# Mixture-of-experts stage: experts ranked by rows on chip, three of them in two products per weight tile, and a seventh of the weight splits on GpSimd

## The chip, the cores and the metric
One core of a Trainium2 chip (trn2). The time is the device time of one execution in microseconds; the kernel before has a median of 1638.44 us over three runs.

## What is computed
The kernel runs a trunk of two layers over 256 rows of 1024 numbers, all in float32. Each layer has an attention, a cross-attention to 256 memory rows and a feed-forward part, each followed by a layer norm of `ALPHA * x + sublayer(x)`. The change lies in the last feed-forward part, the experts of layer 1:

```python
def swiglu(x, w_gate, w_up, w_down):
    return (jax.nn.silu(x @ w_gate) * (x @ w_up)) @ w_down

def moe_swiglu(x, router, w_gate, w_up, w_down):
    logits = (x @ router).astype(jnp.float32)
    top_vals, top_idx = lax.top_k(logits, TOP_K)
    gates = jax.nn.softmax(top_vals, axis=-1)
    combine = jnp.sum(jax.nn.one_hot(top_idx, N_EXPERTS, dtype=jnp.float32) * gates[..., None], axis=-2)
    y = jnp.zeros_like(x)
    for e in range(N_EXPERTS):
        y = y + combine[..., e:e + 1].astype(x.dtype) * swiglu(x, w_gate[e], w_up[e], w_down[e])
    return y
```

There are 8 experts, each row takes the best 2 of them, and an expert has three matrices of 1024 x 3584 (the last one transposed): 44.04 MB in float32.

## The kernel before, in words
**Products in two halves.** A float32 matrix is split into a high half (`hi`, rounded to float32r) and a low half (`lo` = value - `hi`). A product is the sum of three matmuls: x_hi with w_hi, x_hi with w_lo, x_lo with w_hi (L397 to L399).

**Chunks.** Weights come in chunks of 1 MB: 128 partitions x 4 tiles of 512 columns. An expert has EC = 42 chunks: 28 for gate and up (EJ = 7 column blocks, two chunks of gate and two of up each), then 14 for down (7 for each half of y's 1024 columns). For each chunk SP issues the DMA into one of seven `raw` buffers (NEXP = 7; L921, once the low half of the chunk seven earlier is made), ACT makes `w_hi` by a copy (L1116), DVE makes `w_lo` by a subtraction (L1964, `w_split` in DVE's `expert`), and PE runs 12 matmuls of 128x512.

**Slots.** The halves lie in four slots (`E_SLOT`), except for the chunks 20 to 25, which go round in three. `E_SPLIT[c]` lists the chunks whose halves may be made once PE has used chunk c: c + 4, or 3 later near there. ACT waits for `chunk_used`, DVE for `hi_made`, PE for `lo_made`; every engine goes through its own instructions in order.

**Jobs.** One job is one expert; `expert(job, z)` is written once for each engine as the body of a loop and once more, with z = "z", for the last job. A job takes up to 128 rows of its expert; where one expert has more, a second round of 8 jobs follows (`rounds`). The rows are placed by prefix sums (`place`), and a one-hot matrix `pick` (L1855) selects them. At chunk 4 (`C_INDEX`) PE forms the row numbers of the next job, DVE copies them (`got_i`, L1467), POOL gathers the rows (`get_x`, L1077), and at chunk 32 (`C_TURN`) PE turns them and ACT and DVE split them into `xe_hi` and `xe_lo` (L1869). For each column block j ACT computes silu of gate (`e_g`, L1420), DVE multiplies by up (`e_h`, L1957), PE transposes (L864), and ACT and DVE split the result into `eT_hi` and `eT_lo` (L1973). y is copied by ACT and stored by a DMA into `y_rows` (L1432).

**Last job.** DVE works out the row numbers of all rows' two results (`row_numbers`, L1890 to L1907), POOL gathers them from `y_rows` in four pairs (`get_y`, L1086, each pair after DVE has added the one before), and DVE adds them to x (`add_got`, L1932) at the chunks 12, 16, 20 and 24. The last job's own y is combined by PE (L819) and added by DVE (`add_last`, L1941). The final layer norm and the store of the output follow. Its parameters `gb` are loaded by POOL's `ln_params(5)` before the experts.

**GpSimd (POOL).** Ahead of the experts it makes five `w_lo` by the same subtraction (`split`, L1010), masks for the attention (L945) and, in layer 0, fills a part of `y_rows` with x by 10 DMAs of 512 KB so that unused rows hold numbers (L1027).

Of the kernel before, what the change touches and what calls it, by code (L numbers as in the profile page):

```python
# [26 lines left out]
P = 128  # L27
# [4 lines left out]
def trunk(nc, x, mem, ln_g, ln_b, mem_wq, mem_wkv, mem_wo, ab_w_in, ab_sinks, ab_w_out,  # L32
# [77 lines left out]

    with ExitStack() as ctx:
# [88 lines left out]
        eT_lo = at("eT_lo", [P, EK, P], F32R, o_region + 4 * EK * P)  # L200
        o = o_region + 8 * EK * P
# [10 lines left out]
        xe_lo = at("xe_lo", [P, KT, P], F32R, o_xt + 4 * KT * P)  # L212
        e_h = [at(f"e_h{i}", [P, W], F32, o_scr + 4 * W * i) for i in range(2)]
# [9 lines left out]
        for name, shape, dt in (  # L223
# [17 lines left out]
        taken, place, most, rounds = (small[n] for n in ("taken", "place", "most", "rounds"))  # L241
        token_no, got_i, mine, nth, late = (
            small[n] for n in ("token_no", "got_i", "mine", "nth", "late"))
        fin, is_fin, w_fin, last_job = (small[n] for n in ("fin", "is_fin", "w_fin", "last"))
# [39 lines left out]
        for n in range(NSPL + 1, EC + NSPL + 1):  # L284
            at_step = max(at_step, max(m for m in range(-EC, n) if E_SLOT[m % EC] == E_SLOT[n % EC]))
            E_SPLIT[at_step].append(n)
        C_GOT = {12 + 4 * n: (n // TB, n % TB) for n in range(2 * TB)}
        C_INDEX, C_TURN, C_COMBINE = 4, 4 * EJ + 4, 4 * EJ + EK // CK + 2
# [76 lines left out]
        def _(pe):  # L365
            pair = [0]

            def chunk_product(c, outs, lhs_hi, lhs_lo, k0, first, last, cols, idx=None, slot=None,
                              rows=None, done=None, ready=None, turned=False):
# [3 lines left out]
                pe.wait_ge(lo_made, c + 1 if idx is None else idx + 1)  # L373
# [435 lines left out]
            pe.wait_ge(sem("rounds_made"), 2)  # L809
            last = pe.value_load(last_job[0:1, 0:1], min_val=NE - 1, max_val=2 * NE - 1)  # L810
# [12 lines left out]
            def expert(job, z):  # L823
                start = list(claims)
                for c in range(EC):
# [4 lines left out]
                    if c == C_INDEX:  # L830
                        pe.wait_ge(sem("picked"), job + 2)
                        if z:

                            d = claim(pe, "pT", 5, job)
# [3 lines left out]
                        else:  # L838
                            index("iB", job)
                    if c < 4 * EJ:  # L840
                        j, q = c // 4, c % 4
                        key, b = (f"{z}eg{j}", j % 2) if q < 2 else (f"{z}eu{j}", 2 + j % 2)
                        if q % 2 == 0:
                            claim(pe, key, b, job, signal=False)
                        chunk_product(c, [(0, bank[b])], xe_hi, xe_lo, 4 * (q % 2), q % 2 == 0,
                                      q % 2 == 1, W, idx=idx, slot=E_SLOT[c], done=chunk_used)
                    else:
# [3 lines left out]
                        if i == 0:  # L851
# [3 lines left out]
                                      q == EK // CK - 1, W, idx=idx, slot=E_SLOT[c],  # L855
                                      done=chunk_used)
                    if c % 4 == 1 and 1 <= c // 4 <= EJ:
# [5 lines left out]
                        for q in range(4):  # L863
                            m = nc.tensor.transpose(d[:, q * P:(q + 1) * P],  # L864
                                                    e_h[j % 2][:, q * P:(q + 1) * P], ident[:, :])
                        m.then_inc(filled[b], 1)
                    if c == C_TURN and not z:

                        pe.wait_ge(sem("x_got"), 16 * job + 16)
                        turn("xB", job)  # L870
                    if z and c in (C_COMBINE, EC - 1):
# [7 lines left out]
            assert [a - b for a, b in zip(claims, before[0])] == JOB_CLAIMS  # L879
# [6 lines left out]
        def _(sp):  # L886
# [45 lines left out]
            with sp.Else():  # L932
                sp.nop()
# [1121 lines left out]
```

## Time and profile before

| | |
|---|---|
| three runs | 1637.53, 1638.44, 1640.66 us; median 1638.44 |
| profiled execution: span from first to last instruction | 1639.8 us |
| its own time | not listed beside the span; the span stands for it |
| first expert chunk on PE | about 666 us |
| last matmul of the last expert chunk | about 1625 us |
| busy: PE / DVE / ACT / POOL | 1599.7 / 1259.6 / 1029.8 / 121.1 us |
| moved by DMA | 481.24 MB, mean 293 GB/s |

Busy times are sums over the span, and matmuls overlap, so a busy PE only says that it never ran dry. The granted clock of PE is given as a share of full speed: 1.00 is 2.4 GHz, 0.50 is 1.2 GHz. A span of 2.29 us of one DVE instruction contains a start-up that the next one overlaps.

### The profile page before, as it was taken

The numbers are of one execution on the slowest core, as the hardware profiler recorded it, in microseconds if no ns is written. First come the engines' busy times: TensorE is split into PE (matmuls) and PEld (weight loads), VectorE is DVE, ScalarE is ACT, GpSimd is POOL, SyncE is SP. The second block draws the span as 40 slices with busy tenths as digits, with TensorE's granted clock in tenths as the row PEclk, the third lists the DMA queues.
The fourth block names the chain that finished last, engine by engine and source line by source line (L and its number), as shares of the span: only waits on it lengthen the run. The fifth ranks groups of instructions, "written<-read, shape, count | busy, mean of one in ns | idle before, by whom it ended". The sixth has DMA issues, their size and how long they took to land.

```text
span 1639.8 us, 22497 instructions
## 1 busy us (share of the span) xinstructions
PE 1599.7 (98%) x8202; PEld 1347.1 (82%) x8202; DVE 1259.6 (77%) x1173; ACT 1029.8 (63%) x920; POOL 121.1 (7%) x131
## 2 busy tenths in 40 slices
PE   9999999999999998999999999999999999999996
PEld 8888988888896796888888888888888888888775
DVE  4687475554647656889889889888988988988996
ACT  4564444343437454677777777777777777777673
POOL 2103010000104101000000000000000000000120
PEclk9999999999999999999999999999999999999999
DMA  9437656466455363899999999999999999999992
GB/s 351 164 127 252 213 182 216 128 219 200 161 193 185 135 206 105 318 364 377 389 363 385 389 364 375 389 371 384 388 368 387 388 358 386 388 362 389 359 369 94
DMA packets 238397, 481.24 MB, mean 293 GB/s; under 512 B 8256, under 2 KB 11360, under 8 KB 238336
## 3 DMA queue, kind: packets, MB, share of 16 engines
q1 hardware_dynamic: 229744, 454.06, 77.3%
q0 software_dynamic: 6576, 22.68, 4.1%
q10 hardware_dynamic: 2016, 3.67, 0.6%
q8 instruction: 40, 0.66, 0.2%
q14 instruction: 21, 0.17, 0.0%
HBM read 474.07 MB, written 11.56 MB: 296 GB/s over the span
## 4 chain that ended last, share of the span: by engine, by line
PE 84%; DVE 9%; issue 2%; DMA 2%; ACT 2%; POOL 1%; POOLq 0%; DVEq 0%; SPq 0%; ACTq 0%
PE bank L397 23%; PE bank L399 23%; PE bank L398 23%; PE bank L387 3%; PE bank L390 3%; PE bank L389 3%; DVE w_lo L1483 2%; PE bank L864 1%; DVE w_lo L1964 1%; DMA y_got<-y_rows,row_i 1%; PE bank L684 1%; PE bank L660 1%; DVE X L1520 1%; ACT w_hi L1116 1%; DVE X L1529 1%
## 5 line engine op out<-in xcount | busy, mean ns | idle before, releaser
L1116 ACT ACTIVATE w_hi<-raw 128x2048 fp32r<-128x2048 f32 (+1 forms) x322 | 608.8, 1895 | 258.7 <-PE bank L399 220.3
L1964 DVE TENSOR_TENSOR w_lo<-raw,w_hi 128x2048 fp32r<-128x2048 f32 x221 | 503.1, 2290 | 81.8 <-ACT w_hi L1116 78.5
L1483 DVE TENSOR_TENSOR w_lo<-raw,w_hi 128x2048 fp32r<-128x2048 f32 (+1 forms) x96 | 211.2, 2204 | 145.5 <-ACT w_hi L1116 145.2
L397 PE MATMUL bank<-w_hi,xe_hi 128*128 128x512 f32 x736 | 292.9, 398 | 1.2 <-DVE w_lo L1964 1.2
L399 PE MATMUL bank<-w_hi,xe_lo 128*128 128x512 f32 x736 | 287.9, 391 | 0.0
L398 PE MATMUL bank<-w_lo,xe_hi 128*128 128x512 f32 x736 | 287.4, 390 | 0.0
L399 PEld LDWEIGHTS bank<-w_hi,xe_lo 128*128 128x128 f32 x736 | 138.5, 188 | 29.9
L397 PEld LDWEIGHTS bank<-w_hi,xe_hi 128*128 128x128 f32 x736 | 138.6, 188 | 28.8 <-DVE w_lo L1964 1.6
L398 PEld LDWEIGHTS bank<-w_lo,xe_hi 128*128 128x128 f32 x736 | 138.8, 189 | 27.4
L1964 DVE TENSOR_TENSOR w_lo_more<-raw,w_hi_more 128x2048 fp32r<-128x2048 f32 x63 | 144.2, 2290 | 18.5 <-ACT w_hi_more L1116 11.4
L397 PE MATMUL bank<-w_hi,xT_hi 128*128 128x512 f32 (+1 forms) x384 | 147.0, 383 | 0.1
L399 PE MATMUL bank<-w_hi,xT_lo 128*128 128x512 f32 (+1 forms) x384 | 144.5, 376 | 0.0
L398 PE MATMUL bank<-w_lo,xT_hi 128*128 128x512 f32 (+1 forms) x384 | 144.5, 376 | 0.0
L1116 ACT ACTIVATE w_hi_more<-raw 128x2048 fp32r<-128x2048 f32 x64 | 122.9, 1920 | 28.0 <-PE bank L399 23.8
L397 PE MATMUL bank<-w_hi,eT_hi 128*128 128x512 f32 x320 | 125.8, 393 | 0.5 <-DVE w_lo L1964 0.5
L399 PE MATMUL bank<-w_hi,eT_lo 128*128 128x512 f32 x320 | 124.6, 390 | 0.0
L398 PE MATMUL bank<-w_lo,eT_hi 128*128 128x512 f32 x320 | 124.6, 389 | 0.0
L387 PE MATMUL bank<-xT_hi,w_hi 128*128 128x256 f32 x352 | 101.1, 287 | 2.1 <-DVE w_lo L1483 2.1
L389 PE MATMUL bank<-xT_lo,w_hi 128*128 128x256 f32 x352 | 100.3, 285 | 0.0
L390 PE MATMUL bank<-xT_hi,w_lo 128*128 128x256 f32 x352 | 100.3, 285 | 0.0
L1964 DVE TENSOR_TENSOR w_lo<-raw_more,w_hi 128x2048 fp32r<-128x2048 f32 x40 | 91.4, 2286 | 3.7 <-ACT w_hi L1116 3.7
L1116 ACT ACTIVATE w_hi<-raw_more 128x2048 fp32r<-128x2048 f32 x40 | 76.7, 1916 | 25.0 <-PE bank L399 25.0
(291 smaller groups left out, 2598.4 us busy)
## 6 DMA issues: line engine op xcount, KB each, us to landing
raw<-in_moe_w_gate_dram SPq DMA_DIRECT2D x96, 1024.0 KB, 9.2
raw<-in_moe_w_up_dram SPq DMA_DIRECT2D x96, 1024.0 KB, 8.4
raw<-in_moe_w_down_dram SPq DMA_DIRECT2D x96, 1024.0 KB, 7.2
raw<-in_mem_wkv_dram SPq DMA_DIRECT2D x16, 1024.0 KB, 5.1
raw_more<-in_moe_w_up_dram SPq DMA_DIRECT2D x16, 1024.0 KB, 8.7
raw_more<-in_moe_w_gate_dram SPq DMA_DIRECT2D x16, 1024.0 KB, 8.7
raw_more<-in_moe_w_down_dram SPq DMA_DIRECT2D x16, 1024.0 KB, 7.8
raw<-in_c_w_in_dram SPq DMA_DIRECT2D x12, 1024.0 KB, 5.2
```

The lines of the kernel that those rows point to most:

```text
L387: nc.tensor.matmul(d, wh, xh, start=(first and k == 0 and q % 2 == 0), stop=False, skip_group_check=True)
L389: nc.tensor.matmul(d, wh, xl, start=False, stop=False, skip_group_check=True)
L390: m = nc.tensor.matmul(d, wl, xh, start=False, stop=(last and k == n - 1), skip_group_check=True)
L397: nc.tensor.matmul(d, xh, hi[:, k, :], start=(first and k == 0), stop=False)
L398: nc.tensor.matmul(d, xh, lo[:, k, :], start=False, stop=False)
L399: m = nc.tensor.matmul(d, xl, hi[:, k, :], start=False, stop=(last and k == n - 1))
L660: m = nc.tensor.matmul(d[:, t * SEQ:(t + 1) * SEQ], QK[:, 2 * h + k, t * P:(t + 1) * P], MK[:, 2 * h + k, :], start=(k == 0), stop=(k == 1))
L684: m = nc.tensor.matmul(d[:, k * SEQ:(k + 1) * SEQ], MV[:, mb, c:c + P], PT_t[i % 2][:, mb * SEQ:(mb + 1) * SEQ], start=(mb == 0), stop=(mb ...
L864: m = nc.tensor.transpose(d[:, q * P:(q + 1) * P], e_h[j % 2][:, q * P:(q + 1) * P], ident[:, :])
L1116: return nc.scalar.activation(dst, src, ACT.Copy)
L1483: tt(w_lo[s][:, 0:n], raw[c % NRAW][:, 0:n], w_hi[s][:, 0:n].bitcast(F32), ALU.subtract).then_inc(lo_made, 1)
L1964: tt(w_lo[s][:, :], raw_exp[r][:, :], w_hi[s][:, :].bitcast(F32), ALU.subtract).then_inc(lo_made, 1)
```

## The change
Four things change; the arithmetic stays within the same scheme.

1. **Ranking.** The number of rows of each of the experts 1 to 7 is counted and ranked on DVE (`count`, `sort_key`, `above`, `rank`, `ranked`); `room` is 64 rows for the three with fewest and 128 otherwise. If all fit (`most` = 0) there are 8 jobs: expert 0 and two wide ones in a loop (WIDE = 3), then twice a pair of a narrow and a wide job (PAIRS = 2), then the last job, narrow. If one doesn't fit, 8 more wide jobs go ahead. SP reads the experts' numbers from `sorted_e`.
2. **Narrow jobs.** The 64 rows' high and low halves stand side by side in the 128 columns of one stationary tile (`xe_two`, `eT_two`), and a weight tile takes two matmuls, with w_hi and with w_lo. The halves of the result are added afterwards: for gate and up by a product with a folding matrix (`fold`), for y by DVE.
3. **GpSimd** makes `w_lo` of the chunks 5, 12, 19, 26, 33 and 40 of each job (`POOL_SPLITS`), from two tiles in SBUF, with a semaphore of its own.
4. **Around it.** `ln_params(5)` moves behind POOL's last split, `y_rows` is filled whole (16 DMAs of 512 KB, not 10), a narrow y is stored with 64 rows and later, and DVE's `row_numbers` grows.

```diff
+    HP = P // 2
+    NARROW, PAIRS = 3, 2
+    WIDE = NE - NARROW - PAIRS
+    ORDER = [0, 1, 4, 2, 5, 3, 6]
+        POOL_SPLITS = [n for n in range(NSPL + 1, EC) if n % NEXP == NEXP - 2]
@@ PE, chunk_product
-                pe.wait_ge(lo_made, c + 1 if idx is None else idx + 1)
+                pe.wait_ge(*((lo_made, c + 1) if idx is None else split_done(c, job)))
+                    if packed is not None:
+                        d, two = outs[0][1][:, 0:cols], packed(k0 + k)
+                        nc.tensor.matmul(d, two, hi[:, k, :], start=(first and k == 0), stop=False)
+                        m = nc.tensor.matmul(d, two, lo[:, k, :], start=False, stop=(last and k == n - 1))
+                        continue
@@ PE, expert
+                            if narrow:
+                                for src, col in ((e_g[j % 2], q * HP), (e_h[j % 2], W // 2 + q * HP)):
+                                    m = nc.tensor.matmul(d[:, col:col + HP], src[:, q * P:(q + 1) * P],
+                                                         fold[:, :], start=True, stop=True,
+                                                         skip_group_check=True)
-            with pe.Fori(0, last) as job:
-                expert(job, "")
-            expert(last, "z")
+            with pe.Fori(0, wide) as job:
+                expert(job, "", False)
+            with pe.Fori(0, PAIRS) as i:
+                job = pe.snap(wide + 2 * i)
+                expert(job, "n", True)
+                expert(job + 1, "w", False)
+            expert(wide + 2 * PAIRS, "z", True)
@@ SP
-                        sp.wait_ge(lo_made, N0 + c - NEXP + 1 + EC * job)
+                        sp.wait_ge(*split_done(c - NEXP, job))
+            for r in range(NR):
+                e = sp.value_load(sorted_e[0:1, r:r + 1], min_val=0, max_val=NE - 1)
+                expert_chunks(e, more + (r + 1))
@@ POOL
-                        for r in range((NE - 2) * P, 2 * NE * P, SEQ):
+                        for r in range(0, 2 * NE * P, SEQ):
-            ln_params(5)
+            def w_split(n, job):
+                r, s = n % NEXP, E_SLOT[n % EC]
+                pool.wait_ge(hi_made, N0 + n + 1 + EC * job)
+                nc.gpsimd.tensor_tensor(w_lo[s][:, :], raw_exp[r][:, :], w_hi[s][:, :].bitcast(F32),
+                                        ALU.subtract).then_inc(sem("lo_by_pool"), 1)
+            def next_x(job):
+                w_split(POOL_SPLITS[0], job)
                 pool.wait_ge(sem("index_made"), job + 1)
                 pool.sem_inc(sem("x_asked"), 1)
                 get_x()
+                for n in POOL_SPLITS[1:]:
+                    w_split(n, job)
+            late_splits = {0: POOL_SPLITS[1:2], 1: POOL_SPLITS[2:3], 2 * TB - 1: POOL_SPLITS[3:]}
             for g in range(2 * TB):
                 get_y(g)
+                for n in late_splits.get(g, ()):
+                    w_split(n, last)
+            pool.wait_ge(chunk_used, EC * wide + (N0 + 4 * EJ + EC * 2 * PAIRS))
+            pool.dma_start(gb[:, 0, :], ln_g[LNS[5]].partition_broadcast(P)).then_inc(sem("ln_in"), 16)
@@ ACT, expert, narrow
+                            copy(e_g[j % 2][:, :], bank_of(f"{z}eg{j}")[:, :])
+                        copy(e_h[j % 2][:, :], bank_of(f"{z}eu{j}")[:, :]).then_inc(sem("e_hidden"), 1)
+                            nc.scalar.activation(e_act[j % 2][:, :], b[:, 0:W // 2], ACT.Silu)\
+                        act.wait_ge(sem("e_mult"), EJ * n_narrow + j + 1)
+                        copy(eT_two[:, 4 * j:4 * j + 4, 0:HP],
+                             e_mul[j % 2][:, :].rearrange("p (k s) -> p k s", k=4))\
@@ DVE, expert
+                        if n in POOL_SPLITS:
+                            return
+                        copy(y[0:HP, col], b[HP:P, :]).then_inc(sem(f"y_low{i}"), 1)
+                        tt(y[0:HP, col], b[0:HP, :], y[0:HP, col], ALU.add).then_inc(sem(f"y_made{i}"), 1)
+                        tt(e_mul[j % 2][:, :], bank_of(f"{z}et{j}")[:, W // 2:W], e_act[j % 2][:, :], ALU.mult)\
+                        empties(tt(eT_two[:, 4 * j:4 * j + 4, HP:P],
+                                   e_mul[j % 2][:, :].rearrange("p (k s) -> p k s", k=4),
+                                   eT_two[:, 4 * j:4 * j + 4, 0:HP].bitcast(F32), ALU.subtract), f"{z}et{j}")
@@ DVE, turned
+                        tt(xe_two[:, 4 * half:4 * half + 4, HP:P],
```

## Rows read from the trace of the kernel before
**Rows 1.** The page's busy shares, and its chain that ended last, by engine.
```profile
PE 1599.7 (98%) x8202; PEld 1347.1 (82%) x8202; DVE 1259.6 (77%) x1173; ACT 1029.8 (63%) x920; POOL 121.1 (7%) x131
...
PE 84%; DVE 9%; issue 2%; DMA 2%; ACT 2%; POOL 1%; POOLq 0%; DVEq 0%; SPq 0%; ACTq 0%
```

**Rows 2.** Windows: us; PE, PEld, DVE, ACT, POOL busy us (x); PEclk; DMA share; GB/s.
```profile
907.08:1026.09 119.01, 119.01 (x545) 98.62 (x545) 104.79 (x61) 90.19 (x61) 2.67 (x1) 1.00 1.03 376
1499.00:1625.50 126.50, 122.40 (x539) 98.69 (x537) 111.13 (x96) 83.52 (x57) 18.09 (x8) 0.99 0.85 313
```

**Rows 3.** Timeline of PE (start us, us, instruction): every third matmul, first and last.
```profile
938.54 0.39 PE L397 MATMUL bank<-w_hi,xe_hi 128*128 128x512 f32 x1
...
942.62 0.39 PE L397 MATMUL bank<-w_hi,xe_hi 128*128 128x512 f32 x1
```

**Rows 4.** Windows with DMA's share and GB/s, experts first, then the fills of layer 0.
```profile
690.00:720.00 30.00, 30.00 (x139) 24.81 (x138) 27.09 (x18) 22.19 (x16) 1.08 (x1) 1.00 1.05 387
892.00:960.00 68.00, 68.00 (x311) 56.31 (x310) 59.75 (x35) 51.90 (x36) 2.67 (x1) 1.00 1.05 388
...
165.00:180.00 15.00, 15.00 (x122) 14.87 (x122) 7.22 (x4) 7.58 (x6) 0.00 (x0) 1.00 1.03 365
180.00:200.00 20.00, 19.70 (x110) 17.29 (x109) 11.10 (x25) 9.85 (x24) 0.00 (x0) 1.00 0.25 91
```

**Rows 5.** Timeline of DVE in one job.
```profile
974.18 0.68 DVE L1957 TENSOR_TENSOR e_h<-bank,e_g 128x512 f32<-128x512 f32 x1
975.09 2.29 DVE L1964 TENSOR_TENSOR w_lo<-raw,w_hi 128x2048 fp32r<-128x2048 f32 x1 [0.22 <-DVE e_h L1957]
...
997.04 0.69 DVE L1973 TENSOR_TENSOR eT_lo<-bank,eT_hi 128x512 fp32r<-128x512 f32 x1
997.64 4.49 DVE L1964 TENSOR_TENSOR w_lo<-raw,w_hi 128x2048 fp32r<-128x2048 f32 x2
```

**Rows 6.** POOL's splits and DVE's L1520: ns min/median/max by line; timeline of 412 to 418.
```profile
L1010 POOL TENSOR_TENSOR w_lo<-raw,w_hi x5: 4607/4612/4617, 136.6 to 634.3; 128x2048 fp32r<-128x2048 f32 x5
...
L1520 DVE SCALAR_TENSOR_TENSOR X<-X,mean_var,gb x10: 1265/1266/1801, 142.0 to 644.7; 128x1024 f32<-128x1024 f32 x10
...
412.40 4.61 POOL L1010 TENSOR_TENSOR w_lo<-raw,w_hi 128x2048 fp32r<-128x2048 f32 x1 [174.61 <-ACT w_hi L1116]
...
414.33 0.69 DVE L1505 SCALAR_TENSOR_TENSOR X<-X,bank 128x512 f32<-128x512 f32 x1 [7.14 <-PE bank L399]
415.05 0.69 DVE L1509 BATCH_NORM_STATS2 stats<-X 128x6 f32<-128x512 f32 x1
...
416.29 1.80 DVE L1520 SCALAR_TENSOR_TENSOR X<-X,mean_var,gb 128x1024 f32<-128x1024 f32 x1
```

**Rows 7.** POOL's selects by line; timeline of POOL, then DVE, 501 to 505.
```profile
L945 POOL TENSOR_SCALAR_AFFINE_SELECT c_add<-c_add x32: 283/295/2332, 461.9 to 538.8; 128x128 f32<-128x128 f32 x32
...
502.36 2.28 POOL L945 TENSOR_SCALAR_AFFINE_SELECT c_add<-c_add 128x128 f32<-128x128 f32 x2 [1.83 <-DMA c_add<-gate_rows]
...
501.95 2.29 DVE L1483 TENSOR_TENSOR w_lo<-raw,w_hi 128x2048 fp32r<-128x2048 f32 x1 [1.06 <-ACT w_hi L1116]
```

**Rows 8.** Timeline of POOL, then DVE, in the last job: gathers of y.
```profile
1546.43 3.01 POOL L1086 DMA_INDIRECT y_got<-y_rows,row_i  x1 [27.38 <-DVEq L1935]
...
1558.59 3.01 POOL L1086 DMA_INDIRECT y_got<-y_rows,row_i  x1 [6.95 <-DVEq L1935]
...
1569.14 0.75 DVE L1932 SCALAR_TENSOR_TENSOR X<-y_got,g,X 128x512 f32<-128x512 f32 x1 [1.36 <-DMA y_got<-y_rows,row_i]
```

**Rows 9.** Windows of the end, and the chain in order of time from the last matmul.
```profile
1605.00:1610.00 5.00, 5.00 (x24) 4.14 (x23) 4.05 (x3) 4.15 (x3) 0.00 (x0) 1.00 0.21 77
...
1625.22 0.24 PE bank L399
```

**Rows 10.** Windows around the router's stage.
```profile
643.50:647.40 3.90, 0.05 (x1) 0.00 (x0) 3.66 (x10) 0.20 (x1) 0.11 (x1) 0.90 0.34 137
647.40:653.30 5.90, 5.61 (x26) 3.84 (x27) 3.16 (x6) 5.11 (x6) 1.58 (x3) 0.50 0.51 160
```

More of the change, by code:

```diff
@@ L200, in trunk @@
         eT_lo = at("eT_lo", [P, EK, P], F32R, o_region + 4 * EK * P)
+        eT_two = at("eT_two", [P, EK, P], F32R, o_region)
+        e_act = [at(f"e_act{i}", [P, W // 2], F32, o_region + 4 * EK * P + 2 * W * i) for i in range(2)]
+        e_mul = [at(f"e_mul{i}", [P, W // 2], F32, o_region + 4 * EK * P + 4 * W + 2 * W * i) for i in range(2)]
         o = o_region + 8 * EK * P
@@ L821, in combine, with expert @@
                         .then_inc(filled[2 * half + t], 1)
-            def expert(job, z):
+            def expert(job, z, narrow):
+                claims[:], signals[:] = before[0], before[1]
                 start = list(claims)
+                last = z == "z"
                 for c in range(EC):
@@ L845, in expert @@
                         chunk_product(c, [(0, bank[b])], xe_hi, xe_lo, 4 * (q % 2), q % 2 == 0,
-                                      q % 2 == 1, W, idx=idx, slot=E_SLOT[c], done=chunk_used)
+                                      q % 2 == 1, W, idx=idx, slot=E_SLOT[c], done=chunk_used, job=job,
+                                      packed=(lambda k: xe_two[:, k, :]) if narrow else None)
                     else:
@@ L1391, in turned @@
                     b = wait_filled(act, f"{tag}{half}", job)
+                    if job is not None:
+                        copy(xe_two[:, 4 * half:4 * half + 4, 0:HP],
+                             b[:, :].rearrange("p (k s) -> p k s", k=4)[:, :, 0:HP])
                     copy(xe_hi[:, 4 * half:4 * half + 4, :].rearrange("p k s -> p (k s)"), b[:, :])\
@@ L1396, in _, with expert @@
             split(N0 + NSPL)
-            act.wait_ge(sem("rounds_made"), 2)
-            last = act.value_load(last_job[0:1, 0:1], min_val=NE - 1, max_val=2 * NE - 1)
+            act.wait_ge(sem("jobs_made"), 2)
+            wide = act.value_load(n_wide[0:1, 0:1], min_val=WIDE, max_val=WIDE + NE)
             assert cursor[0] == N0 + NSPL + 1
-            def expert(job, z):
+            def expert(job, z, narrow, n_narrow=None):
+                last = z == "z"
                 nc.scalar.preload_act_table_set("silu_and_others")
@@ L1945, in add_last, with last_picks, expert @@
                 link(ins)
-            def expert(job, z):
+            def last_picks():
+                for t in range(TB):
+                    for a in (0, HP):
+                        ins = nc.vector.tensor_scalar(pick[:, t, a:a + HP], slot_no[:, 0:HP],
+                                                      place[:, t, 3 * NE - 1:3 * NE], None, ALU.is_equal)
+                ins.then_inc(sem("picked"), 1)
+            def expert(job, z, narrow, n_narrow=None):
+                last = z == "z"
                 for c in range(EC):
                     idx = N0 + c + EC * job
-                    if c < 4 * EJ and c % 4 == 3:
+                    if not narrow and c < 4 * EJ and c % 4 == 3:
                         j = c // 4
@@ L1977, in expert @@
                     if c == 0:
[L1979 to L1980 removed]
+                        if last:
+                            last_picks()
+                        else:
+                            picks(bass.ds(job + (NE + 1), 1))
+                    if c == C_INDEX + 1 and last:
                         b = wait_filled(dve, "pT", job)
```

302 lines of the change are left out of this document (216 added, 86 removed).

## Prediction
> **What bounds the kernel now.** I read the page's shares first: PE is busy for 98% of the span, DVE for 77% [rows 1], and PE has 84% of the chain that ended last [rows 1]. Stages differ, so next the windows: from 668 us on the experts run, one job (one expert) like the other, 119.01 us each. In one such job PE has no idle time, DVE is busy 104.79 us, ACT 90.19, POOL 2.67, and DMA moves 376 GB/s at a share of 1.03 [rows 2]. So PE sets the pace, but DVE has only 14 us to spare. The matmul rows give PE's price: 18 of them in 4.08 us, 0.227 each [rows 3]; 12 a chunk and 42 chunks are 114.4 us, the rest of the 119 are transposes. The third limit is DMA. Over long stretches in which every buffer is asked for as soon as it is free, it moves 387 to 388 GB/s at a share of 1.05, and no longer stretch shows more [rows 4]. A job needs 44.0 MB of weights, 0.5 MB of gathered x and 0.5 MB of stored y: 45.1 MB / 388 GB/s = 116.2 us. DMA is thus 3 us a job behind PE. Three limits lie at 119, 116 and 105 us; the change lowers the first by far and moves the last.
>
> **Does it do what it says?** Worked through the reference with its inputs, the experts get 67, 65, 53, 55, 61, 62, 80, 69 rows. The three smallest of experts 1 to 7 (53, 55, 61) fit into 64 rows and the rest into 128, so there are again 8 jobs, in the order wide, wide, wide, narrow, wide, narrow, wide, narrow. A count too large would add 8 jobs; it isn't so here.
>
> **PE, narrow jobs.** 8 matmuls in place of 12 a chunk: 42 x 8 x 0.227 = 76 us, and with 56 products by fold and the turn about 84, against 119. From PE alone three such jobs would give back 105 us. None of it counts below the next limit: 44.8 MB (half a y) / 388 = 115.5 us by DMA.
>
> **DVE and POOL.** Every job gives 6 of its 42 w_lo splits to POOL. On DVE one costs 2.20 us back to back (two in 4.49, one in 2.29) [rows 5]; on POOL 4.61 us, five of five [rows 6]. As work beside DVE this would take 6 x 2.20 = 13 us from DVE. But the rows speak against "beside". While POOL's split ran from 412.40 to 417.01, a DVE operation with two SBUF inputs (L1520) that began at 416.29 took 1.80 us, where the other nine took 1.27: it ended 1.08 us after POOL did. The two just before it, with an input from a bank or with one input, kept their 0.69 [rows 6]. The other way round, POOL's selects of c_add have a median of 0.295 us but up to 2.33, and a pair took 2.28 us while a w_lo of DVE ran from 501.95 to 504.24, the first of them waiting until that was over [rows 7]. So an operation that reads two SBUF tiles and one of POOL that reads SBUF exclude each other for their whole length; w_lo reads raw and w_hi, both in SBUF. This is how the Trainium skill has it (SBUF — State Buffer, "Who interferes with whom"): VectorE's second input comes through the interface that GpSimd uses, and whoever starts second is blocked until the first is done; these rows agree. By that rule the sum is the one below; without it, it is rival A's.
>
> The price in DVE's stream: from the end of one w_lo POOL needs 4.61 less the 0.19 that a blocked operation has already behind it (1.27 - 1.08), 4.42, and the next w_lo ends 2.10 later; that is 6.52 for what took 4.40, +2.12 us a split, +12.7 a job. The offload costs DVE's stream time instead of giving it any. Wide job: 104.8 + 12.7 + 0.7 (two xe_two parts) = 118.2 us against PE's 119.0. Narrow: 36 x 2.20 + 6 x 4.33 = 105.2; e_mul and eT_two, 128x256 each, in place of e_h and eT_lo of 128x512, which hold the stream for 0.91 and 0.60 [rows 5]: half the columns, some 0.34 each, 14 of them 4.8; turn 1.9; y's low half by copy and add 3.2; picks and index 0.6: 115.7, with a few tenths of waiting 117, beside DMA's 115.5. ACT, with the same 42 splits and some halves more, stays near 95.
>
> **Where waits appear.** A split starts when PE has used the chunk 4 earlier (3 earlier for chunks 23 to 28). Wide, 4 slots: 1.9 (ACT) + 4.6 + 0.2 = 6.7 us within 3 x 2.72 = 8.2, mostly covered, with DVE's lag behind it down to some tenths. Wide, 3 slots (chunk 26, POOL's): 6.8 within 2 x 2.72 + 0.5 (transposes) = 5.9: PE waits 0.9 us a job, where DVE's split fits (4.4). Queued behind DVE's blocked w_lo are e_h and eT_lo, which PE's transposes wait for.
>
> **The sum against the span.** (a) Router: DVE has 6 more small linked operations at 0.2 us before its next split and 9 after the first ones, the latter under PE's first chunks: +0.5; bounds 0 and +3. (b) Jobs 0 to 2, wide: 120.0 each, +3; bounds 0 (all covered) and +12 (DVE's lag reaches PE in each cycle of seven). (c) First narrow: 117, and PE, which ends a wide job 3.8 us behind its last w_lo, ends this one 2 behind: 115.2, -3.8; twice, -7.6; bounds -18 (more of POOL's time under DVE's bank operations, DMA's 115.5 the limit, the full lead given back) and +2. (d) The two wide jobs between start without lead: 119.0 + 0.9 + some 1.6 until the lead is there, +2.5 each, +5; bounds 0 and +8. (e) Last job, narrow: before, 126.5 us, DVE busy 111.1 of them [rows 2] and, in its own order, occupied from the first split to the last. To its stream of 116.4 come 12.7 for POOL, some 13 row-number operations (+2.8), from it go 5.6 (e_h, eT_lo): 126.3. POOL is also asked for y_got here; between two gathers now stands a split. The gathers already follow each other at 12 us, and DVE once waited 1.36 for one [rows 8]; adding 4.6 to that chain costs 2 to 5 us. 131, +4.5; bounds -2 and +10. (f) From the last matmul to the end: 14.3 us [rows 9], unchanged; the layer norm's gb is now fetched behind POOL's last split, 9 us ahead of its use; bounds 0 and +2. (g) Six more y_rows fills early (10 of 512 KB before): DMA is full there until 180 us and then falls to a share of 0.25 [rows 4], and the weights run six buffers ahead: 0; bounds 0 and +3. POOL issues them in 3.4 us, and its next work waited 4.2.
> Sum: 0.5 + 3 - 7.6 + 5 + 4.5 = +5.4. The span of 1639.8 gives 1645.2; the three runs' median of 1638.4 lies 1.4 below that span, so 1643.8, rounded to 1644.
>
> **Rivals.** A, POOL works beside DVE (its w_lo doesn't hold back DVE's): then DVE has 92 us a job, the narrow ones run at DMA's pace and PE's lead over the landing data (DMA falls silent near 1606, PE works to 1625 [rows 9]), 19 us down to 7, is given back once: first narrow -15.5, second -6.3, last -7.7, wide ones +5, router +0.5: -24, 1614. For it: only one pair with POOL's split overlaps in this trace; against it: that pair, and the selects that waited [rows 7]. B, exclusion holds but is absorbed, since 118.2 is still under 119.0 and 115.7 under it too: wide 0, narrow -9.2 and -4, wide between +0.9 each, last +0.5: -11, 1627. It decides if PE's idle time in the wide jobs stays under 0.3 us. C, heavier: every POOL split holds up PE by 0.5 us in wide jobs (5 x 3), narrow jobs gain nothing, last +10: +25 and more, 1664. To it belongs the clock: after 3.9 us without matmuls PE ran at a granted 0.50, that is 1.2 of 2.4 GHz, for 6 us [rows 10]; in narrow jobs PE pauses some 2.5 us at each POOL split, and at that level a chunk needs 3.6 us instead of 1.8. The sign between my case and B hangs on two or three us of stalls, so neither is remote.
>
> **Numbers.** My case 0.46, B 0.22, A 0.15, C 0.12, the small rest between A and B. The range reaches from just under A to the lower part of C: 1613 to 1657; my case alone is 1639 to 1651. A measurement of this kernel can tell 0.2% (3.3 us) from no change: faster (under 1635.2) 0.36, from A, B and the rest; same 0.20, from the edges of my case and B; slower 0.44.
>
> **What would show it.** Right: DVE rows of w_lo with up to 6.7 us beside POOL's 4.6, POOL rows above 4.61 where a w_lo ran, narrow jobs of about 117 us with PE's matmuls near 70% of them, wide jobs of 120, PE waiting for POOL's w_lo. Wrong: w_lo staying at 2.29 us during POOL's splits (A); narrow jobs clearly under 114 us, which would say that DMA can move over 388 GB/s; wide jobs of 123 or PEclk falling in the narrow ones (C).

## The result, and the profile after

Median of four runs 1691.74 us (1690.04 to 1694.52) against 1637.99 (1636.16 to 1640.66) for the kernel before on the same chip: ratio 1.0329, interval 1.0311 to 1.0347. The change makes the kernel 3.3% slower. The profiled execution has a span of 1688.8 us. The forecast of 1644, its range up to 1657 and even rival C (1664) were all too low.

The page of after, shares and chain [rows 1]:

```profile
PE 1558.9 (92%) x7950; PEld 1298.1 (77%) x7950; DVE 1297.8 (77%) x1176; ACT 1040.5 (62%) x972; POOL 362.2 (21%) x196
...
PE 50%; issue 22%; DVE 15%; POOL 7%; ACT 4%; DMA 1%; ACTq 0%; DVEq 0%; POOLq 0%
```

PE has 252 matmul records fewer and yet fell from 98% to 92% of a longer span; its share of the last chain fell from 84% to 50%. DVE lost 48 of its w_lo operations to POOL and is busy 38 us *more* (1297.8 against 1259.6; the same kernel without POOL's splits, experiment 1, has 1261.4). The same in windows, one for each job (columns as in [rows 2]; the jobs are wide, wide, wide, narrow, wide, narrow, wide, narrow, as the prediction worked them out):

```profile
663.40:792.09 128.69, 123.50 (x549) 101.64 (x548) 108.49 (x67) 91.00 (x64) 32.91 (x7) 0.97 0.92 331
...
916.71:1041.31 124.60, 121.11 (x545) 99.71 (x545) 106.36 (x57) 90.88 (x63) 32.91 (x7) 0.99 1.00 362
1041.31:1165.74 124.43, 101.02 (x456) 78.84 (x456) 112.67 (x59) 92.05 (x76) 30.41 (x7) 0.93 0.99 359
1165.74:1295.42 129.68, 124.05 (x549) 101.22 (x547) 110.36 (x61) 91.15 (x64) 33.39 (x7) 0.97 1.01 362
```

A wide job that took 119.01 us now takes 124.6: PE is idle for 3.5 of it, and its 545 matmuls are busy for 121.1 where they were for 119.0, mostly by a slower clock, shown below; a narrow job, with a third fewer matmuls on its weights (456 of all kinds against 545), takes 124.4 and leaves PE idle for 23. Nothing is at its limit there: DMA moves 359 GB/s where it could move 387 [rows 4], DVE is busy 113 us of 124. It is waits. After's lines by source say how the operations changed (ns min/median/max):

```profile
L2179 DVE TENSOR_TENSOR w_lo<-raw,w_hi x189: 2274/2283/6662, 669.6 to 1663.5; 128x2048 fp32r<-128x2048 f32 x189
...
L2179 DVE TENSOR_TENSOR w_lo<-raw_more,w_hi x40: 2276/3919/5436, 676.0 to 1646.8; 128x2048 fp32r<-128x2048 f32 x40
...
L1169 POOL TENSOR_TENSOR w_lo<-raw,w_hi x32: 4516/4624/6124, 669.0 to 1664.9; 128x2048 fp32r<-128x2048 f32 x32
...
L1992 DVE TENSOR_SCALAR pick<-slot_no,place x16: 273/280/4600, 655.0 to 1429.8; 128x128 f32<-128x128 f32 x16
```

The first three are the exclusion as predicted: w_lo up to 6.66 us beside POOL, POOL up to 6.12 beside w_lo. The fourth was not predicted: a comparison of 128 columns that takes 0.28 us takes up to 4.60. Where it stands, in the timeline of a wide job:

```profile
922.17 4.79 DVE L1992 TENSOR_SCALAR pick<-slot_no,place 128x128 f32<-128x128 f32 x2
...
922.29 4.57 POOL L1169 TENSOR_TENSOR w_lo<-raw,w_hi 128x2048 fp32r<-128x2048 f32 x1 [14.76 <-ACT w_hi L1210]
...
926.88 2.28 DVE L2179 TENSOR_TENSOR w_lo<-raw_more,w_hi 128x2048 fp32r<-128x2048 f32 x1
...
927.09 0.60 PE L835 MATMUL bank<-token_no,pick 128*128 128x1 f32 x4 [2.68 <-DVE pick L1992]
```

The picks of chunk 0 (the next job's rows) are issued right behind the w_lo of chunk 4, and POOL's first split of a job, chunk 5, starts 0.12 us after them. The second pick waits until POOL is done, and in PE's queue the index product sits ahead of the experts' matmuls: PE waits 2.68 us. Two microseconds later the granted clock is at 0.50, which is where most of the 2.1 us of longer matmuls come from (with the picks moved, experiment 3, it is 119.5 at a clock of 1.00):

```profile
929.00:931.00 2.00, 2.00 (x6) 1.56 (x5) 1.77 (x3) 0.00 (x0) 0.00 (x0) 0.50 1.05 386
```

In a narrow job PE is further ahead:

```profile
1046.77 4.73 DVE L1992 TENSOR_SCALAR pick<-slot_no,place 128x128 f32<-128x128 f32 x2
...
1051.63 1.01 PE L835 MATMUL bank<-token_no,pick 128*128 128x1 f32 x4 [5.82 <-DVE pick L1992]
```

and the granted clock falls, windows of the same job:

```profile
1051.00:1056.00 5.00, 4.37 (x12) 3.67 (x13) 4.90 (x3) 0.17 (x1) 0.42 (x1) 0.50 1.05 388
1056.00:1061.00 5.00, 5.00 (x26) 4.26 (x25) 2.29 (x1) 3.60 (x3) 0.00 (x0) 0.74 1.05 387
```

After 5.8 us without a matmul of the experts PE runs at 0.50, that is 1.2 GHz, as after the 3.9 us of [rows 10], and does 12 matmuls in 5 us. PE's waits from 700 to 1670 us (us in total, times, longest):

```profile
PE bank L420 <- DVE w_lo L2179: 24.3, 18, 4.5
PE bank L835 <- DVE pick L1992: 21.5, 6, 5.8
PE bank L420 <- POOL w_lo_more L1169: 9.3, 6, 2.3
PE bank L420 <- DVE eT_two L2195: 9.0, 3, 3.0
PE bank L420 <- DVE w_lo_more L2179: 7.0, 2, 6.5
PE bank L881 <- DVE pick L2142: 6.1, 1, 6.1
...
PE bank L439 <- POOL w_lo L1169: 4.0, 5, 0.8
```

L420 is the narrow jobs' first product, L439 the wide ones'. In before the longest entry of this view is 2.3 us in all. The first entry, 24.3 us, is for the most part not the splits' doing: without them (no_pool) it is still 18.9 us in 18 waits. The pick's 21.5 us are 1.8 there.

### The profile page after: what moved, and what is told of

Read it like the earlier page. It is cut to its first block, busy times and chain, and to the rows that moved or that the text cites. A ratio compares the mean times of both kernels' runs of the same rounds, so it can differ in the third digit from the quotient of the medians.

```text
span 1688.8 us, 22163 instructions
## 1 busy us (share of the span) xinstructions
PE 1558.9 (92%) x7950; PEld 1298.1 (77%) x7950; DVE 1297.8 (77%) x1176; ACT 1040.5 (62%) x972; POOL 362.2 (21%) x196
## 4 chain that ended last, share of the span: by engine, by line
PE 50%; issue 22%; DVE 15%; POOL 7%; ACT 4%; DMA 1%; ACTq 0%; DVEq 0%; POOLq 0%
PE bank L439 11%; PE bank L441 11%; PE bank L440 11%; DVE w_lo L2179 4%; POOL w_lo L1169 3%; PE bank L429 3%; PE bank L432 3%; PE bank L431 3%; ACT w_hi L1210 2%; POOL w_lo_more L1169 2%; DVE w_lo L1620 2%; PE bank L420 1%; DVE w_lo_more L2179 1%; PE bank L421 1%; DVE pick L1992 1%
## 5 line engine op out<-in xcount | busy, mean ns | idle before, releaser
L2179 DVE TENSOR_TENSOR w_lo<-raw,w_hi 128x2048 fp32r<-128x2048 f32 x189 | 440.0, 2351 | 62.2 <-ACT w_hi L1210 59.8
L1169 POOL TENSOR_TENSOR w_lo<-raw,w_hi 128x2048 fp32r<-128x2048 f32 x32 | 157.3, 4916 | 404.2 <-ACT w_hi L1210 404.2
L439 PE MATMUL bank<-w_hi,xe_hi 128*128 128x512 f32 x460 | 186.6, 406 | 4.0 <-POOL w_lo L1169 4.0
L441 PE MATMUL bank<-w_hi,xe_lo 128*128 128x512 f32 x460 | 182.8, 397 | 0.0
L440 PE MATMUL bank<-w_lo,xe_hi 128*128 128x512 f32 x460 | 182.7, 397 | 0.0
L439 PE MATMUL bank<-w_hi,xT_hi 128*128 128x512 f32 (+1 forms) x384 | 147.0, 383 | 0.1
L420 PE MATMUL bank<-w_hi,xe_two 128*128 128x512 f32 x276 | 120.4, 436 | 18.1 <-DVE w_lo L2179 10.7
L1169 POOL TENSOR_TENSOR w_lo_more<-raw,w_hi_more 128x2048 fp32r<-128x2048 f32 x16 | 81.3, 5081 | 212.6 <-ACT w_hi_more L1210 212.6
L421 PE MATMUL bank<-w_lo,xe_two 128*128 128x512 f32 x276 | 115.3, 418 | 0.9 <-issue 0.9
L439 PEld LDWEIGHTS bank<-w_hi,xe_hi 128*128 128x128 f32 x460 | 88.7, 193 | 22.9 <-POOL w_lo L1169 5.2
L441 PEld LDWEIGHTS bank<-w_hi,xe_lo 128*128 128x128 f32 x460 | 88.5, 192 | 19.4
L440 PEld LDWEIGHTS bank<-w_lo,xe_hi 128*128 128x128 f32 x460 | 88.8, 193 | 17.8
```

The lines of the kernel that those rows point to most:

```text
L420: nc.tensor.matmul(d, two, hi[:, k, :], start=(first and k == 0), stop=False)
L421: m = nc.tensor.matmul(d, two, lo[:, k, :], start=False, stop=(last and k == n - 1))
L439: nc.tensor.matmul(d, xh, hi[:, k, :], start=(first and k == 0), stop=False)
L440: nc.tensor.matmul(d, xh, lo[:, k, :], start=False, stop=False)
L441: m = nc.tensor.matmul(d, xl, hi[:, k, :], start=False, stop=(last and k == n - 1))
L1169: nc.gpsimd.tensor_tensor(w_lo[s][:, :], raw_exp[r][:, :], w_hi[s][:, :].bitcast(F32), ALU.subtract).then_inc(sem("lo_by_pool"), 1)
```

## Experiments

Two theories. **Theory 1**: POOL's splits cost the time, because POOL and DVE keep each other out of SBUF; the narrow products alone are a gain. **Theory 2**: the rest of the change (ranking, narrow jobs, their order on DVE) costs it. Ratios are to the kernel before on the same chip.

**1. no_pool**: after, with no split on POOL.

```
-POOL_SPLITS = [n for n in range(NSPL + 1, EC) if n % NEXP == NEXP - 2]
+POOL_SPLITS = []
```

> The changed kernel with all low halves of the experts on DVE again; ranking and narrow jobs stay. Theory 1 (POOL's splits and DVE's two-input operations exclude each other, and that is what the change costs): DVE's w_lo rows are all 2.29 us, the first narrow job takes about 116 us by DMA less some lead, the wide ones 119, and the time falls from 1691.7 to about 1614 us, under the kernel before. Theory 2 (the narrow form costs: its longer chain ACT-DVE-PE, pauses and PE's clock): narrow jobs stay at 123 us or more and the time stays over 1660.

Measured: 1616.97 us (1614.99 to 1619.18), ratio 0.9857, interval 0.9839 to 0.9874. Two of its jobs, wide and narrow, in windows:

```profile
904.32:1023.38 119.06, 119.06 (x546) 98.63 (x545) 105.45 (x63) 90.73 (x63) 2.68 (x1) 1.00 1.03 376
1023.38:1133.88 110.50, 100.57 (x472) 78.82 (x471) 103.51 (x67) 93.12 (x75) 2.54 (x1) 0.97 1.05 388
```

Wide jobs are back at 119.06, PE without a gap; the narrow one ends at DMA's 388 GB/s. Six splits more on DVE, and DVE is busy 9 us *less* in the narrow job than in after. The change without POOL's splits is worth 1.4%; the splits cost 4.8% beside it (1.0329 / 0.9857).

**2. before_pool**: the kernel before, plus POOL's six splits of a job and nothing else of the change. The first stands ahead of the gather of x and the rest behind it, DVE passes these chunks over, and PE and SP wait for whoever makes a chunk.

```
+                w_split(POOL_SPLITS[0], job)
...
+                for n in POOL_SPLITS[1:]:
+                    w_split(n, job)
...
+                        if n in POOL_SPLITS:
+                            return
```

> The kernel before with nothing but POOL's six splits a job. Theory 1: each wide job costs what it costs in the changed kernel, 124.6 us in place of 119.0, eight jobs give +45 and with the gathers of the last one some +50: about 1685 us. Theory 2: within 5 us of the kernel before, 1638.

Measured: 1687.09 us (1680.33 to 1697.63), ratio 1.0302, interval 1.0253 to 1.0351. The splits cost the old kernel 3.0%. Its jobs 1 to 4 take 123.0 us instead of 119.0, jobs 5 and 6 124.6, the last 138.4 instead of 123.3. Two of these jobs in windows:

```profile
911.08:1034.07 122.99, 119.50 (x546) 98.58 (x545) 105.09 (x55) 90.36 (x61) 32.30 (x7) 1.00 1.01 367
1280.01:1404.60 124.59, 121.12 (x545) 99.74 (x545) 105.05 (x55) 90.37 (x62) 32.26 (x7) 0.99 1.00 362
```

PE waits 16.0 us in six for the picks, 2.7 each. After the same 2.7 us the granted clock stayed at 1.00 in the first of the two and fell to 0.50 in the second, which makes it 1.6 us longer; why it fell in one and not in the other no run shows. The time met the expected 1685, but not by its sum: the expectation had 124.6 for every wide job, five of seven had 123.0, and the last job lost 15.1 us, more than was put down for it. Theory 2 falls, as it does by experiment 1. Alone the splits cost 3.0%, beside the narrow jobs 4.8%.

**3. picks_first**: after, with the picks of chunk 0 ahead of the w_lo of chunk 4 on DVE, to keep them away from POOL's split. Is the pick a tenth of the loss or most of it?

```
+                    if c == 0:
+                        if last:
+                            last_picks()
+                        else:
+                            picks(bass.ds(job + (NE + 1), 1))
                     if not narrow and c < 4 * EJ and c % 4 == 3:
...
-                    if c == 0:
-                        if last:
...
```

> The changed kernel with DVE's picks of chunk 0 ahead of w_lo of chunk 4 in place of behind it, so that they are not queued beside POOL's split of chunk 5. In the profile of the changed kernel the picks take 4.8 us in place of 0.48 and PE waits 2.7 (wide) to 5.8 us (narrow) for them. Theory 1a (the picks are the main place of the cost): PE's waits at the index are gone, with the slow clock behind them, 5 x 3 + 3 x 8 us: about 1655 us. Theory 1b (DVE's stream is full, so the stall only moves to the next operation behind the split): at most 10 us faster, 1682 or more.

Measured: 1662.73 us (1660.98 to 1666.32), ratio 1.0135, interval 1.0119 to 1.0152. The placement of two operations of 0.28 us a job is worth some 30 of the 75 us between after and no_pool (the ratios give 1.9%). A wide and a narrow job:

```profile
912.66:1032.93 120.27, 119.46 (x545) 98.49 (x545) 106.76 (x57) 90.90 (x63) 34.92 (x7) 1.00 1.02 375
1032.93:1149.17 116.24, 99.69 (x454) 77.33 (x454) 108.66 (x58) 92.14 (x75) 32.34 (x7) 0.96 1.04 380
```

120.27 and 116.24, where the prediction had 120.0 and 115.2. The time still lies 8 us over 1a's value. One reason is that the move does not clear the picks everywhere: in jobs 0 and 4 the first pick meets POOL's split all the same and takes 4.18 and 4.69 us, and PE waits 2.1 and 1.9. What else is left stands in the table below.

**4. before_pool_picks**: the same move in the version of experiment 2, where nothing of the narrow jobs disturbs the reading.

> The kernel before with GpSimd's six splits (1687) and VectorE's picks of chunk 0 issued ahead of its low half of chunk 4. Theory 1a (the picks, held for GpSimd's split of chunk 5, keep TensorE 2.7 to 3 us a job, and that is most of what a split costs a wide job): jobs of 120.0 in place of 123.0, over eight jobs about 24 less, 1658 to 1668. Theory 1b (the low halves that are late cost the time, whoever is blocked first): over 1678.

Measured: 1657.09 us (1655.45 to 1662.59), ratio 1.0121, interval 1.0097 to 1.0145: 1a, a touch under its band. Here no pick takes over 0.29 us. Jobs 1 to 6 take 120.2 or 120.3 us each:

```profile
905.56:1025.82 120.26, 119.45 (x546) 98.50 (x545) 105.46 (x55) 90.37 (x62) 34.28 (x7) 1.00 1.03 374
```

So a wide job's 4.0 us were 2.8 for the picks and 1.2 for all six splits together; the last job, 132.5 us instead of 123.3, still pays 9.2. Over the run the 48 splits cost 18 us here (1657.1 against 1639.1), 0.4 each.

**5. half**: after, with three splits a job on POOL (chunks 12, 26, 40), none near the picks.

```
+POOL_SPLITS = [12, 26, 40]
...
                 get_x()
-                for n in POOL_SPLITS[1:]:
+                for n in POOL_SPLITS:
```

> The kernel after, but GpSimd makes the low halves of chunks 12, 26 and 40 alone (three a job in place of six, none of them near the picks of chunk 0, and each behind the gather of x). Theory 1c: each split of GpSimd costs the same wherever it stands, because for its 4.6 us it and VectorE's low halves keep each other out; between the version without them (1617) and the one with six and the picks moved ahead (1663) three lie in the middle: about 1640 (1633 to 1648), VectorE's low halves beside them about 6.7 us, and no pick over 0.6 us. Theory 2c: it is the split of chunk 5, close behind the start of the job, that does the harm, and VectorE has slack for the others: 1617 to 1627.

Measured: 1637.97 us (1633.8 to 1641.74), ratio 0.9989, interval 0.9976 to 1.0002. With 0, 24 and 48 splits (the last with the picks moved) the medians are 1617.0, 1638.0 and 1662.7: 0.88 and 1.03 us a split. Theory 1c's time came, and of the numbers tried none is free: with three a job all that the narrow jobs bring is spent. Its reason, the same cost wherever a split stands, did not: against no_pool the three splits cost a wide job 1.0 us, the first narrow job 2.5 and the last job 7.3 (table below), and in the kernel without narrow jobs a split cost 0.4 (experiment 4).

**6. pool_writes and pool_copy**: what in POOL's operation keeps DVE out? In the first POOL fills its six w_lo with zeros (it writes and reads nothing); in the second it copies raw to w_lo (one input). Both leave the subtraction out for six chunks of 42.

```
-nc.gpsimd.tensor_tensor(w_lo[s][:, :], raw_exp[r][:, :], w_hi[s][:, :].bitcast(F32), ALU.subtract)...
+nc.gpsimd.memset(w_lo[s][:, :].bitcast(F32), 0.0)...
```

```
-nc.gpsimd.tensor_tensor(w_lo[s][:, :], raw_exp[r][:, :], w_hi[s][:, :].bitcast(F32), ALU.subtract)...
+nc.gpsimd.tensor_copy(w_lo[s][:, :], raw_exp[r][:, :])...
```

> Leaves out the subtraction of POOL's six chunks a job: their w_lo is set to zero by a POOL instruction that writes the same tile and reads nothing. Theory 1 (the exclusion is at SBUF's read side): DVE's w_lo rows stay at 2.29 us while POOL writes, and the time falls to about 1620. Rival (any POOL operation holds DVE's two-input ones back): w_lo rows of 2.29 plus the length of POOL's write, up to 4 us or more, remain.

> The kernel after, with GpSimd's six subtractions replaced by copies of the raw chunk to w_lo (it reads one input and writes; the subtraction of the high half is left out for six chunks of 42). Theory 3a (any fp32 operation of GpSimd that reads SBUF takes turns with VectorE's of two inputs): low halves of 4.5 us and more beside it on VectorE and a time from 1640 to 1690. Theory 3b (only two inputs at once do that): low halves of 2.29 us throughout and about 1613, as with the fills of zero.

Measured: 1613.31 us (one run) and 1619.92 us (1617.5 to 1620.4, ratio 0.9879, interval 0.9861 to 0.9896). The same three places in both timelines, first pool_writes:

```profile
791.05 2.12 DVE L1992 TENSOR_SCALAR pick<-slot_no,place 128x128 f32<-128x128 f32 x2
...
791.25 1.84 POOL L1170 MEMSET w_lo<- 128x2048 f32 x1 [18.50 <-ACT w_hi L1210]
...
1511.78 1.80 POOL L1170 MEMSET w_lo<- 128x2048 f32 x1 [7.07 <-ACT w_hi L1210]
1511.83 2.29 DVE L2179 TENSOR_TENSOR w_lo_more<-raw,w_hi_more 128x2048 fp32r<-128x2048 f32 x1
...
1532.39 0.43 DVE L2195 TENSOR_TENSOR eT_two<-e_mul,eT_two 128x256 fp32r<-128x256 f32 x1 [0.48 <-ACT eT_two L1210]
1532.40 1.82 POOL L1170 MEMSET w_lo_more<- 128x2048 f32 x1
```

then pool_copy:

```profile
790.06 2.20 DVE L1992 TENSOR_SCALAR pick<-slot_no,place 128x128 f32<-128x128 f32 x2
...
790.27 1.91 POOL L1170 CAST w_lo<-raw 128x2048 fp32r<-128x2048 f32 x1 [18.15 <-ACT w_hi L1210]
...
1514.71 1.89 POOL L1170 CAST w_lo<-raw 128x2048 fp32r<-128x2048 f32 x1 [7.07 <-ACT w_hi L1210]
1514.74 4.00 DVE L2179 TENSOR_TENSOR w_lo_more<-raw,w_hi_more 128x2048 fp32r<-128x2048 f32 x1
...
1536.87 2.20 DVE L2195 TENSOR_TENSOR eT_two<-e_mul,eT_two 128x256 fp32r<-128x256 f32 x1 [0.48 <-ACT eT_two L1210]
1536.89 1.90 POOL L1170 CAST w_lo_more<-raw 128x2048 fp32r<-128x2048 f32 x1
```

Two rules, not one. An operation of DVE with two SBUF inputs is undisturbed by POOL's writes (2.29, 0.43) and waits out POOL's reads, though the copy reads one input only (4.00 = 1.9 + 2.1; 2.20). The pick, with one tensor input, waits for either (2.12, 2.20 for two that take 0.48). 3a is right that one input is enough, but its size was not met: it had w_lo of 4.5 us and more, and the longest is 4.00, all but a few staying at 2.29. By its time 3b was nearer. The likely reason is that a copy of 1.9 us is mostly over before DVE's next w_lo is due, a chunk being 2.7 us; this was not tested by itself. The expectation tied the mechanism and the time together, wrongly. This is how the Trainium skill has it (SBUF — State Buffer, "Who interferes with whom"): two SBUF inputs contend with GpSimd's reads alone, while tensor_scalar is among the operations that can use both port pairs, when its operands meet certain conditions, and then contends with GpSimd. The runs agree with the first half, at these numbers. With the second they agree in that the pick waits for a GpSimd operation that only writes; in which mode the pick ran no trace shows.

**7. unrolled, picks_first_unrolled**: the loop over pairs of jobs has a body of two jobs. At its jump back, in every version with it, ACT stands still, for 3.7 to 4.0 us; the loop over one job shows no such gap. Here picks_first:

```profile
1280.14 1.28 ACT L1501 ACT_TABLE_LOAD   x1 [3.71 <-issue]
1281.20 0.19 PEld L421 LDWEIGHTS bank<-w_lo,xe_two 128*128 128x128 f32 x1 [1.15 <-issue]
```

The edit, for PE, POOL, ACT and DVE, once in no_pool and once in picks_first:

```
-with act.Fori(0, PAIRS) as i:
+for i in range(PAIRS):
```

> The version without GpSimd's splits (1617.0), with the loop over the two pairs of a narrow and a wide job written out for TensorE, GpSimd, ScalarE and VectorE, so that nothing jumps back between the pairs. Theory L (the jump back over a body of two jobs costs ScalarE 3.8 us without an instruction, and TensorE 2.5 us and 3 us at half clock): the ScalarE gap at the second pair is under 1 us and the time 3 to 6 us shorter, 1611 to 1614. Theory M (the gap is code loading that straight code has too, or the transfers bound these jobs anyway): 1616 to 1618, with the gap still there or given back to the transfers.

> The kernel after with the picks ahead of the low half of chunk 4 (1662.7) and the loop over the two pairs of jobs written out for four engines. Without GpSimd's splits the jump back cost nothing, because the transfers bound those jobs. Theory L2 (with the splits the transfers are behind, so the 3.7 us gap of ScalarE at the jump back, which sits in a wide job of 131.0 where 121.6 is usual, is on the path): that job falls to 125 or less and the time to 1654 to 1659. Theory M2 (the gap is hidden here too, and what is long are VectorE's low halves behind GpSimd's): 1661 to 1665 with that job still at about 131.

Measured: 1617.01 us (1615.74 to 1618.66), ratio 0.9863, interval 0.9846 to 0.9879; and 1659.48 us (1657.9 to 1660.86), ratio 1.0121, interval 1.0104 to 1.0138. In both profiles the gap of ACT is gone. In no_pool it bought nothing (M): the job that ends at the jump fell from 121.4 us to 117.7, the next rose from 112.0 to 115.1, and DMA ran at 387 to 388 GB/s in both before. In these jobs, which run at DMA's pace, the stall costs nothing. In picks_first the job that had 131.0 us has 122.0, as L2 said, but the narrow job ahead of it has 119.2 instead of 116.2, and the total is 3.2 us less, between L2 and M2, with intervals of the ratios that overlap. The job of 122.0 also lost its late pick (4.69 us before, under 0.3 now), so the 9 us aren't the jump's alone. That the jump back costs 3 us there is possible and not settled.

**8. no_pool_picks**: the picks moved in no_pool.

> The version without GpSimd's splits (1617.0), with the picks of chunk 0 ahead of the low half of chunk 4. Its picks take 0.28 us each, and TensorE waits 3.2 us for them in all (two of the narrow jobs) and 1.8 us in the last job. Theory R (the order of the picks matters alone beside GpSimd's splits, because the transfers bound the narrow jobs and TensorE the wide ones): 1617 within 2. Theory Q (those waits are on the path): 1612 to 1614.

Measured: 1615.56 us (1614.76 to 1616.64), ratio 0.9855, interval 0.9838 to 0.9871, the same as no_pool within what can be told (R). PE's wait at L835 is gone and nothing follows from it. no_pool is thus the version to keep, 1.4% under before and 1.0329 / 0.9857 = 4.8% under after; no other run that computes everything was measurably faster.

## Why the prediction was wrong, by its own steps

Lengths of the jobs in us, from the start of one on ACT to that of the next, the last to its last matmul (forecast: the terms (a) to (e) on before's own lengths):

```
job            before  forecast  after  picks_first  half   no_pool
0 wide          119.9    121.4   128.7     126.4     121.6   120.5
1 wide          119.0    120.0   124.6     120.3     120.1   119.1
2 wide          119.0    120.0   124.6     120.3     120.1   119.1
3 narrow        119.0    115.2   124.4     116.2     113.0   110.5
4 wide          119.0    121.5   129.7     131.0     125.3   121.4
5 narrow        119.0    115.2   123.4     119.7     113.3   112.0
6 wide          119.0    121.5   125.7     121.6     121.3   118.5
7 narrow, last  123.3    127.8   130.0     128.8     124.1   116.8
```

Before summing: after's first job started 4.8 us earlier than before's, for no reason that the change gives; in the profiles of the other versions it started between 662.7 and 666.8, in the two that are before with splits at 665.0 and 664.4. So of the span's 1688.8 - 1645.2 = 43.6 us over the forecast the jobs hold 48.4: some 16.5 in jobs 0 to 2, 17.4 in the two narrow ones, 12.4 in the two wide ones between and 2.2 in the last.

**What held.** The kind and order of the jobs. The exclusion read from [rows 6, 7], both ways: rival A's condition failed (its time, 1614, came true only where POOL reads nothing, 1613.3). That the offload gives DVE no time: 105.5 us busy in a wide job with six operations fewer, against 104.8. The term (b) of 120.0 for a wide job: 120.3 once the picks were out of the way, with PE waiting 0.8 us at a POOL split where 0.9 was forecast. The narrow job of 115.2: 116.2, in picks_first. The 387 to 388 GB/s as DMA's limit, and the 14.3 us of (f).

**Right numbers by a wrong road.** The +2.12 us a split, +12.7 a job in DVE's stream did not come. With the picks clear DVE is busy 105.5 us in a wide job of before_pool_picks and 106.8 in one of picks_first, where the prediction had 118.2; in the first narrow job it is 108.7 where it had 115.7. The sum let POOL begin at the end of one w_lo with the next one already due. In the trace DVE is often waiting for ACT's w_hi at that moment: in the wide job shown of picks_first it idles 1.80 us and its w_lo then takes 5.02 where 6.66 is the whole block. The 120.0 of (b) rests on the wait at chunk 26, worked out by itself, and stands. The 115.2 of (c) rests on the stream of 117 and was met by luck: PE there waits 9.5 us in six for POOL's w_lo itself.

**The step that failed** is "picks and index 0.6" in the account of DVE's stream. It counts the picks as free of POOL, because the prediction drew from [rows 6] that an operation with one SBUF input keeps its time. That row is a BATCH_NORM_STATS2; the pick is a TENSOR_SCALAR of 128 columns. The trace of before had two rows of that operation beside POOL, neither used in the prediction:

```profile
416.02 0.15 DVE L1517 TENSOR_SCALAR var_eps<-mean_var 128x1 f32<-128x1 f32 x1
...
504.36 0.37 DVE L1680 TENSOR_SCALAR P<-P,row_inv 128x128 f32<-128x128 f32 x1
...
L1680 DVE TENSOR_SCALAR P<-P,row_inv x24: 285/286/369, 65.2 to 541.4; 128x128 f32<-128x128 f32 x24
```

The first, of one column, stands beside POOL's split of 412.40 and keeps its 0.15 us. The second, of 128 columns, begins 0.28 us before POOL's pair of selects of [rows 7] ends, at 504.64, and takes 0.37 where the median is 0.286: it ends 0.09 after the pair. That was a sign, of under 0.1 us. The pick waits out POOL's whole split, up to 4.60 us for 0.28, and it stands, in DVE's order, just where POOL's split of chunk 5 begins. The step "queued behind DVE's blocked w_lo are e_h and eT_lo" looked at one queue only: DVE's. In PE's, the index product stands ahead of the matmuls, and so the pick is as urgent as a w_lo. Undone, this gives back some 30 us in after (experiment 3) and 30 in before_pool (2 and 4), the slower clock behind these waits included. The medians miss by 48 us (1691.7 against 1644): it is some three fifths of that. The rest is in the terms that follow, and not all of it is taken apart.

**The sum's other terms**, by what experiment 3 leaves: 1662.7 against 1644.

- (a), the router, +0.5 with a bound of +3: the first job has 126.4 where 121.4 was forecast. Neither the tail of the router alone (no_pool, 120.5) nor the splits alone (before_pool_picks, 121.0) do this, and half, whose first split is of chunk 12, has 121.6. Together they do: after the nine linked operations DVE is late, and POOL's split, asked for at once, goes first. In after it holds up a w_lo and the picks behind it (PE waits 4.4 us for them), in picks_first the first pick itself:

```profile
668.20 0.23 DVE L2056 SCALAR_TENSOR_TENSOR place<-place,most 128x14 f32<-128x14 f32 x1
...
669.01 4.57 POOL L1169 TENSOR_TENSOR w_lo<-raw,w_hi 128x2048 fp32r<-128x2048 f32 x1 [23.01 <-ACT w_hi L1210]
...
669.59 6.15 DVE L2179 TENSOR_TENSOR w_lo<-raw,w_hi 128x2048 fp32r<-128x2048 f32 x1 [1.15 <-ACT w_hi L1210]
```

  (after; below, picks_first)

```profile
671.71 4.58 POOL L1169 TENSOR_TENSOR w_lo<-raw,w_hi 128x2048 fp32r<-128x2048 f32 x1 [24.30 <-ACT w_hi L1210]
672.20 4.37 DVE L1992 TENSOR_SCALAR pick<-slot_no,place 128x128 f32<-128x128 f32 x2 [1.17 <-issue]
```

  The two edits were priced one by one and not as neighbours.
- (d), the wide job behind the first narrow one, 121.5: 131.0. PE lost its lead to a narrow job, a pick is held here too (PE waits 1.9 us for it), and the jump back of the loop falls at its end (PE waits 2.4 us without a releaser). Some of it is in no_pool (121.4) and half (125.3) too. The prediction had no term for the loop's own body growing to two jobs; how its excess divides between jump, lost lead, pick and splits stays open.
- (c), the second narrow job, 115.2: 119.7; the first held.
- (e), the last job, +4.5: in after +6.7, inside its bounds.

**The rivals.** C, heavier, named the right places (PE held up in each job, the clock at 0.50 in the narrow ones, 1051 to 1056 us) at half the price (+25 against +49 between the two spans): it put 0.5 us at every split of a wide job, where the loss was one wait of 2.7 us there with the clock falling behind it, and of 5.8 in a narrow job, at one operation. The fall of the clock in wide jobs, 1.6 us each, is in no rival. B needed PE's idle time in wide jobs under 0.3 us; it was 3.5. The bounds of the sum were set term by term around the one mechanism, and in after (c), at +9.8 for the two, is over its +2, and (d), at +17.4, over its +8; nothing in them stood for an operation put down as unaffected, and the range was that much too narrow.

## What to carry to other kernels

Before work is moved to GpSimd, list every operation of VectorE that can fall beside it, the small ones too, and ask of each how it reads, and of the moved one whether it reads SBUF at all: here moving an fp32 subtraction of two SBUF tiles saved VectorE nothing (1267.2 us busy in before_pool, 1259.6 in before), where a fill in its place did (1167.6 against 1261.4 in no_pool). Then look in the *consumer's* queue: an operation of 0.3 us that the matmul engine's in-order queue waits for is worth its blocked length, not its own. A change made of two ideas is best read with each alone: one was worth -1.4%, the other +3.0%, and the two together +3.3%, which is worse than their product of +1.5%.

## What the runs showed of the hardware that was not expected

- A TENSOR_SCALAR of 128 columns on VectorE waits for all of GpSimd's operation, whether that reads two inputs (up to 4.60 us), copies (2.20 for two) or only writes (2.12 for two); one of a single column did not wait beside a split (0.15, as always); a TENSOR_TENSOR with two SBUF inputs waits for GpSimd's reads and not for its writes (2.29 beside a fill of 1.80).
- The price of one split of 128x2048 given to GpSimd, taken over whole runs, is 0.9 to 1.0 us of kernel time beside the narrow jobs and 0.4 without them (experiments 5 and 4, the picks moved), though GpSimd is idle for 79% of after's span.
- After waits of TensorE of the same 2.7 us the granted clock stayed at 1.00 in four jobs of before_pool and fell to 0.50 in two; there the fall costs 1.6 us of a job (123.0 and 124.6).
- A jump back over a body of two jobs stalls ACT for 3.7 to 4.0 us without an instruction; written out, the stall is gone. In the stretch of no_pool that DMA bounds that stall costs nothing (1616.97 us with it, 1617.01 without).
